# A third pair per group of the second matrix by seven products, and sums inside a PSUM bank, in a two-layer encoder trunk

## What is computed

```python
def sq_relu_mlp(y, w_up, w_down):
    u = y @ w_up
    return jnp.square(jax.nn.relu(u)) @ w_down
# per layer: h = h + sq_relu_mlp(rmsnorm(h, g), mlp_w_up[i], mlp_w_down[i])
# w_up is 1024 x 4096, w_down is 4096 x 1024
```

## Time and profile before

| | |
|---|---|
| median of 3 runs | 1188.13 us (1187.54 to 1189.15) |
| the profiled execution, its own time | 1189.99 us |
| its span | 1188.3 us |
| granted TensorE clock, mean | 0.997 |
| PE busy | 1175.8 us, 99% |
| DVE busy | 968.3 us, 81% |
| ACT busy | 740.9 us, 62% |
| POOL busy | 160.6 us, 14% |
| feed-forward part of layer 0 | 250.6 to 597.0 us of the span |
| feed-forward part of layer 1, but for the last two pairs | 839.5 to 1155.6 us |

### The profile page before, as it was taken

One profiled execution on the slowest core, in us unless ns is written; L12 is line 12 of the kernel. 1 busy time (PEld: TensorE's weight loads), 2 busy tenths in 40 slices (PEclk: granted clock), 3 DMA queues, 4 the chain that ended last, 5 costly groups with the idle time before them and its releaser, 6 DMA issues.

```text
span 1188.3 us, 23190 instructions
## 1 busy us (share of the span) xinstructions
PE 1175.8 (99%) x8809; PEld 1125.7 (95%) x8809; DVE 968.3 (81%) x1567; ACT 740.9 (62%) x1257; POOL 160.6 (14%) x227
## 2 busy tenths in 40 slices
PE   9999999999999999999999999999999999999998
PEld 8999999999999999999999999987799999989978
DVE  6889888788888888887568989887988788898853
ACT  6777877745555564654357887877655556655643
POOL 3211120100120120221010000000101201202100
PEclk9999999999999999999999999999999999999999
DMA  7343342446596696697232122314467967859832
GB/s 179 95 111 87 89 106 80 141 120 148 116 212 145 124 211 161 133 194 202 68 98 63 55 70 71 88 45 128 132 150 144 196 161 149 188 135 201 210 105 72
DMA packets 233241, 153.92 MB, mean 130 GB/s; under 512 B 25224, under 2 KB 216768, under 8 KB 233152
## 3 DMA queue, kind: packets, MB, share of 16 engines
q1 hardware_dynamic: 214400, 104.94, 32.5%
q0 software_dynamic: 18624, 47.68, 21.1%
q10 hardware_dynamic: 128, 0.09, 0.0%
HBM read 111.43 MB, written 19.24 MB: 110 GB/s over the span
## 4 chain that ended last, share of the span: by engine, by line
PE 70%; issue 19%; DMA 5%; DVE 2%; ACT 2%; POOL 1%; SPq 0%; DVEq 0%; POOLq 0%; ACTq 0%
PE ps L2387 26%; PE ps L2310 19%; PE ps L2075 18%; PE ps L2605 2%; DMA raw<-in_mlp_w_down_dram 2%; PE ps L2130 1%; DMA lo<-raw 1%; DMA raw<-in_mlp_w_up_dram 1%; PE ps L2148 1%; DMA xin<-in_x_dram 1%; DMA h_sum<-abuf 1%; PE ps L2262 0%; PE ps L2216 0%; ACT hi L784 0%; ACT wh L784 0%
## 5 line engine op out<-in xcount | busy, mean ns | idle before, releaser
L2075 PE MATMUL ps<-yh,wh 128*128 128x264 f32 (+1 forms) x704 | 160.5, 302 | 0.0
L2075 PE MATMUL ps<-yl,wh 128*128 128x264 f32 (+1 forms) x704 | 155.3, 295 | 0.0
L2075 PE MATMUL ps<-yh,wl 128*128 128x264 f32 (+1 forms) x704 | 155.3, 295 | 0.0
L784 ACT ACTIVATE hi<-lof 128x1024 fp32r<-128x1024 f32 x80 | 82.9, 1052 | 92.3 <-DVE lof L1650 92.3
L784 ACT ACTIVATE hi<-raw 128x1024 fp32r<-128x1024 f32 (+1 forms) x128 | 116.2, 913 | 20.8 <-DMA raw<-in_mlp_w_down_dram 20.8
L2387 PE MATMUL ps<-th,hi 128*128 128x264 f32 (+1 forms) x448 | 126.6, 283 | 0.0
L2387 PE MATMUL ps<-tl,hi 128*128 128x264 f32 (+1 forms) x448 | 126.4, 282 | 0.0
L2387 PE MATMUL ps<-th,lo 128*128 128x264 f32 (+1 forms) x448 | 126.3, 282 | 0.0
L2310 PE MATMUL ps<-ah,hi 128*128 128x264 f32 (+1 forms) x448 | 116.5, 318 | 2.6 <-DVE al L1721 2.4
L2310 PE MATMUL ps<-al,hi 128*128 128x264 f32 (+1 forms) x448 | 116.2, 318 | 0.0
L2310 PE MATMUL ps<-ah,lo 128*128 128x264 f32 (+1 forms) x448 | 116.0, 317 | 0.0
(11 more groups left out here) (334 smaller groups left out, 3313.3 us busy)
## 6 DMA issues: line engine op xcount, KB each, us to landing
raw<-in_mlp_w_up_dram SPq DMA_DIRECT2D x64, 512.0 KB, 5.6
raw<-in_mlp_w_down_dram SPq DMA_DIRECT2D x64, 512.0 KB, 5.1
lo<-raw POOLq DMA_DIRECT2D x28, 512.0 KB, 5.5
raw<-in_diff_w_in_dram SPq DMA_DIRECT2D x24, 512.0 KB, 3.7
raw<-in_mlstm_w_in_dram SPq DMA_DIRECT2D x16, 512.0 KB, 4.7
lo<-raw POOLq DMA_DIRECT2D x28, 256.0 KB, 3.8
h_sum<-abuf POOLq DMA_DIRECT2D x24, 264.0 KB, 5.1
h_sum<-abuf POOLq DMA_DIRECT2D x24, 256.0 KB, 5.2
```

The costliest lines, as they stand in the source:

```text
L784: return nc.scalar.activation(o, i, ACT.Copy, scale=scale)
L2075: last = mm(ps[:, bank + s, 0:w_], w[:, slot, kb, :], m[:, kb, t0:t0 + w_], start=(kb == 0 and n == 0), stop=(kb == CB - 1 and n == 2))
```

## The change

1. Pair 5 of groups 0 to 2 is crossed as well: 23 crossed pairs a layer.
2. The order of the products is A11, A12, S2, S1, S3, S4, A22. A11, S2, S3 and A22 add up in one bank (matmuls that go on with `start` false), and ScalarE copies the bank after each of the first three (`snap` into `t1`, `u2`, `u3`). TensorE waits for the copy before the next product of that bank. Even and odd pairs have four banks each.
3. VectorE has four sums a pair, and three of them write into the bank they read. `relu` reads PSUM. For second-matrix pairs ScalarE's `send` copies from PSUM into `ab`, where VectorE's sums wrote there before.
4. The lists are written anew: in VectorE's, `block_lo` of S3 and S2 is in pair 4, of S1 and A22 in pair 5; the ends of pair i - 1 come before the low parts for pair i + 1; the forms S2 and S4 of pair i + 2 stay last.

```diff
+FIRST_DOWN = 5
 def crossed_down(i):
-    return 0 <= i < PAIRS - 8 and i % 8 >= 6
+    return 0 <= i < PAIRS - 8 and i % 8 >= FIRST_DOWN
...
-PRODUCTS = ("A11", "A12", "S2", "S3", "S1", "S4", "A22")
+PRODUCTS = ("A11", "A12", "S2", "S1", "S3", "S4", "A22")
...
-SUMS = {"C11": 1, "U2": 2, "U3": 3, "C22": 4, "U4": 5, "C12": 6, "C21": 7}
+SUMS = {"C11": 1, "U4": 2, "C22": 3, "C12": 4}
+SNAPS = {"A11": 1, "S2": 2, "S3": 3}
+USER = {"A11": "C11", "S2": "U4", "S3": "C22"}
+BANK = {"A11": 0, "S2": 0, "S3": 0, "A22": 0, "S1": 1, "A12": 2, "S4": 3}
...
 def bank_of(i, name):
-    return place_of(i, name) % 8
+    return 4 * (i % 2) + BANK[name]
...
-                def snap(i):
-
-                    act.wait_ge(m_done, items + DONE[i, "A11"])
-                    wait(act, c_done, 7 * (ranks + RANK[i] - 1) - 7 + SUMS["U2"])
-                    copy(t1[:, 0:w], ps[:, bank_of(i, "A11"), 0:w]).then_inc(t1_done, 1)
+                def snap(i, name):
+
+                    act.wait_ge(m_done, items + DONE[i, name])
+                    if ranks + RANK[i] > 1:
+                        act.wait_ge(c_done, 4 * (ranks + RANK[i] - 2) + SUMS[USER[name]])
+                    to = {"A11": t1, "S2": u2, "S3": u3}[name]
+                    copy(to[:, 0:w], ps[:, bank_of(i, name), 0:w]).then_inc(snap_done, 1)
...
                     if name == "C11":
+                        dve.wait_ge(snap_done, snaps + snapped(i, "A11"))
                         dve.wait_ge(m_done, items + DONE[i, "A12"])
-                        dve.wait_ge(t1_done, ranks + RANK[i])
-                        o, x, y = to[0][:, first], t1[:, 0:w], p("A12")
+                        o, x, y = p("A12"), t1[:, 0:w], p("A12")
...
+                    before = {"S2": "A11", "S3": "S2", "A22": "S3"}
+                    if name in before:
+                        pe.wait_ge(snap_done, 3 * ranks + snapped(i, before[name]))
...
-                                      start=(kb == 0 and n == 0), stop=(kb == 3 and n == 2))
+                                      start=(name not in before and kb == 0 and n == 0), stop=(kb == 3 and n == 2),
+                                      skip_group_check=name in before)
```

More of the change, by code:

```diff
@@ L119 @@
 SENT_LOW = counted((i, e) for i in range(PAIRS) if by_dma(i) for e in ("A1", "A22"))
-PLAINS = counted((i, m) for i in range(PAIRS) if not crossed(i) for m in range(2))
+UP = counted((i, m) for i in range(PAIRS) if is_up(i) for m in range(2))
+DOWN = counted((i, m) for i in range(PAIRS) if not is_up(i) for m in range(2))
 RANK = counted(i for i in range(PAIRS) if crossed(i))
-UPS = counted(i for i in range(PAIRS) if crossed(i) and is_up(i))
 SENT = counted(i for i in range(PAIRS) if sent_down(i))
@@ L481, in plain_out, with crossed_out, relued, sent @@
             return ps[:, b:b + 2, 0:HALF] if layer == 0 else ps[:, b, 0:X]
+        def crossed_out(layer, i, m):
+            b = unit_bank(i, m)
+            return ps[:, b:b + 2, 0:mlp_shape(layer)[1]]
+        def relued(layer, i, m):
+            return N_UP * layer + UP[i, m]
+        def sent(layer, i, m):
+            return N_DOWN * layer + DOWN[i, m]
         def first_k(i):
@@ L1159, in mlp @@
                         split_unit(U_IN1 + 1, 1, 1, 0)
-                    if crossed(i) and is_up(i):
-                        squares(i, 0)
                 if layer == 0:
@@ L1672, in total @@
                 def total(i, name):
-                    base = 7 * (ranks + RANK[i] - 1)
+                    base, snaps = 4 * (ranks + RANK[i] - 1), 3 * ranks
                     p = lambda product: ps[:, bank_of(i, product), 0:w]
-                    first, second = slice(t0, mid), slice(mid, T)
-                    to = ab if crossed_down(i) else tb
-                    if name in ("C11", "C22"):
-                        m = int(name == "C22")
-                        if crossed_down(i):
-                            wait(dve, h_sent[m], sent_before(layer, i))
-                        else:
-                            wait(dve, ah_done, block_of(i, m) - 1)
@@ L1844, in mlp @@
                         total(i, "C12")
-                    if after:
-                        form(i + 2, "S2", 1)
                     if crossed(i) and is_up(i):
@@ L1849, in mlp @@
                     if after:
+                        form(i + 2, "S2", 1)
                         form(i + 2, "S4", 3)
```

253 lines of the change are left out of this document (117 added, 136 removed).

## The result

The changed kernel takes **1237.8 us** (median of 4 runs, 1231.2 to 1239.0) beside 1188.0 for the kernel before in the same job (1187.5 to 1189.2): a ratio of **1.041, 95% interval 1.037 to 1.044**. It is slower, as forecast, but by 49.8 us and not by 21, and it lies outside the range of 1199 to 1218.

The account below looks back on a forecast made before the run. TensorE, busy 1175.8 of 1188.3 us, bounds the kernel. The terms -8.1 + 24.9 + 8.4 - 4.7 sum to +20.5 us, taking the median from 1188.13 to 1209 us; range 1199 to 1218.

Parts of the forecast that it names:

- The copies: ScalarE's bank copies in seven-product pairs: 0.9 us spare each, so TensorE loses nothing, 0 us.
- the clock: TensorE's clock falls once after each of six long waits, 1.4 us each: 8.4 us more.
- the block waits: Pair 5: TensorE waits for VectorE's late forms at S2 and S1, 3.95 us in layer 0, 4.35 in layer 1: 24.9 more.
- the old waits: Earlier TensorE waits for `al` and `abuf`, with one clock fall, go: 4.7 us less.
- One of its own signs of being wrong: The forecast is wrong if no group waits over 2 us, or if waits appear in first-matrix pairs.
- The gain of pair 5, -8.1: Pair 5 of three groups in each layer goes from plain to seven products: 8.1 us less.
- The stated upper end, 16.8: Upper end for TensorE's clock loss: two falls after each of six long waits, 16.8 us.
- Rival 2: ScalarE, held by late weights, makes copies delay TensorE 0.2 us in each of 46 pairs: 9 us more, 1218; chance 0.13.
- "Nothing for either" queue: Weight loads land 5.1 us later, before first read, and GpSimd issues sends in time: no cost.

Follow-up runs that it names:

- experiment 3: The changed kernel with each second-matrix send cut to 16 tokens (output leaves out the rest): 1217.6 us, ratio 1.023.
- experiment 5: The changed kernel with pair 5 plain again and each second-matrix send cut to 16 tokens: 1201.6 us, ratio 1.010.
- experiment 4: The changed kernel with VectorE's `block_lo` of S1 ahead of pair 6's low part and forms, and ScalarE's S2 copy ahead of a high part: 1233.6 us.
- experiment 6: The changed kernel with block forms, sums and some ScalarE copies moved earlier in the lists, full sends: 1231.3 us, ratio 1.034.
- Experiment 16: The kernel before, with one low part of pair 29's weights moved behind the second low part of pair 27's activations: 1184.7 us, ratio 0.9956.
- experiment 13: The changed kernel with the sends of pairs 7, 15 and 23 issued only once the next load has landed: 1235.6 us, ratio 1.039.
- experiment 14: The changed kernel with pair 5 plain again and sends of pairs 7, 15 and 23 held until the next load has landed: 1223.7 us, ratio 1.028.
- experiment 11: The changed kernel with pair 5 plain again, VectorE's sums ahead of forms, and copies of A11 and S2 earlier in pairs 9, 17, 25: 1220.3 us.
- experiment 15: experiment 11 with the sends of pairs 7, 15 and 23 issued only once the next load has landed: 1222.3 us, ratio 1.027.
- experiment 7: experiment 6 with the sends cut to 16 tokens (output leaves out the rest): 1199.1 us, ratio 1.008.

## Why the prediction was wrong

The sign, the place and the form of the main loss were right; the sum was 29 us short. In the span it forecast 20.5 and got 47.9. The copies make 17.0 of the difference, the clock and the edges of the waits 8.5, the block waits 2.6, the late start 1.3, and the old waits take back 1.8. One of its own signs of being wrong came true: waits in first-matrix pairs. By its own steps:

- **The gain of pair 5, -8.1:** no run isolates it. The spacing it rests on held: in experiments 3 and 5, as in the changed kernel, crossed pairs 2 and 3, which have no wait, run at 0.121 and 0.118 a matmul.
- **The block waits, +24.9:** 27.5 measured. S1 of 3.34 to 3.36 was forecast at 3.38 and 3.35. S2 came to 1.03 and 1.45, not 0.57 and 1.0. VectorE's chain ended 0.33 later (`blocks_r` for S2 ends at 312.04, 15.49 after pair 4's start at 296.55), and some 0.1 of landing is in each. For layer 1 its own terms give 0.88 at S2 and not 1.0, a slip of little weight. Experiments 4 and 6 show the mechanism.
- **The old waits, -4.7:** 6.5 measured. Experiment 16 prices the `al` waits and the fall behind them at 5.2 by themselves; the forecast had 3.8 for these.
- **The clock, +8.4:** mis-sized. Eight falls at 1.4 to 2.7 us, 15.4 in all, not six at 1.4. Three block waits brought a fall of double length, and three of the eight followed waits for copies, which the forecast did not have. The stated upper end, 16.8, holds, though by another count of falls. The Trainium skill, "TensorE: Matmul & The Clock Gate", section "What's actually happening", says that activity is what releases the throttle. The trace agrees at these eight places, each with a wait beside it; yet the waits of 1.45 and 3.36 us that ended at 923.65 and 928.49 left the clock at 1.00.
- **The copies, 0: this is the step that failed.** "I take nothing", from the copy's own 0.9 us of room in the middle of a layer. Measured: 17.0 us, and the falls behind three of them. Rival 2 named the mechanism, ScalarE held by late weights with a copy behind it, but priced it as 0.2 us in each of 46 pairs, with a chance of 0.13. It is 0.5 to 2.8 us in eight pairs, all the second or third of the first-matrix pairs that follow on a group's second-matrix pairs. The earlier trace rows had shown a wait of 5.06 us for such a load; the copies should have been laid behind that row, as the block forms were laid behind VectorE's.
- **"Nothing for either" queue:** also wrong. Loads were taken to land in 5.1 us. At the group's border they took 6.0 to 7.3 even before and take 9.2 to 11.4 now, and experiments 13 and 14 show that the sends beside them are most of the reason. The Trainium skill, "DMA: Bandwidth & Descriptors", section "Issuing engines are not separate DMA queues", says that transfers from all issuing engines run on the same 16 DMA engines and interleave. The trace agrees: with the sends away, the same load takes 7.7 us.

So the 17 us of copies need two things at once: a load slowed by what is issued beside it, sends above all, and copies queued behind the work on that load. Cutting the sends takes the waits for `t` nearly all away (15.7 to 1.7), by an earlier issue of the loads and by shorter ones. Moving the copies in the lists takes a part (experiment 11: 34.0 us of waits to 26.3). Moving the sends mostly moves them (15.7 to 13.8 in experiment 13).

**What stays open.** Why GpSimd's and SyncE's issues meet in the changed kernel and not before was not taken apart: the sends now wait for ScalarE's copies, where VectorE's sums released them, and a late load makes the next low part and the sends late with it. That this feeds itself is an argument from the timelines of experiment 11 and not shown by a run. With 16-token sends the load for pair 10 still took 8.7 us (343.37 to 352.09), and in experiments 13 to 15 loads with a low part close by took some 2 us more than the others. No run moves the low parts by themselves, so their share is read from these places and not shown. The clock falls at some waits and not at others of the same length; what decides it is open too.

## What to carry to other kernels

When an operation is put between two uses of a bank, its price is not its length against the room it has on average. It is the latest transfer that its engine's list waits for ahead of it, at every place where the stages change; go through those places first. A moved send is a moved load on the queues: note what else is issued within some 2 us of it, which in these runs cost a load 2 to 6 us. And a wait that is ordered away at one product should be looked for at the next; here it came back at the next product or pair three times.

## What the runs showed of the hardware

- One transfer of weights, two of 512 KB, takes 7.0 us to land with sends 2.6 and 4.2 us behind it, 10.0 with them within 2 us, 12.9 with a low part and both sends within 2.5 us. The traffic is the same in all three. With no send near it takes 6.1 to 7.7, and 8.0 to 10.1 if a low part is issued within 1.3 us of it (experiments 13 to 15).
- Sums that read and write a PSUM bank take 0.43 to 0.44 us for 264 elements, as those that write SBUF did: where the result goes costs nothing to be seen.
- A wait of over 3 us does not always bring the half clock: five of the six at S1 did. In experiment 7, six waits of 1.40 to 1.76 us brought none, where the earlier trace rows had a fall after 1.64. In experiment 6, each of the three waits of 1.77 us at S2 of pair 5 in layer 1 was followed by one (granted clock 0.51 to 0.52 from 923.4, 1015.4 and 1104.2 on).
